# Matmul order in two places: column groups in turn for the first conditioning blocks, row halves in turn for the state-space outputs

## The chip, the core and the metric

The kernel runs on one core of one Trainium2 chip. The metric is the device time of one execution in microseconds (us). An engine runs its own list of instructions in order and waits on semaphores for the others: TensorE (PE, matmuls; its weight loads are listed apart as PEld), VectorE (DVE), ScalarE (ACT), GpSimd (POOL) and SyncE (SP, which starts DMAs).
## The reference

Two layers work on 512 latent tokens and 256 context tokens of 1024 channels. Nine modulation vectors per layer come from a conditioning vector, for latent and for context:

```python
mod_lat = (silu(c) @ w_ada[l] + b_ada[l])        # 9 vectors of 1024
mod_ctx = (silu(c_ctx) @ w_ada[l] + b_ada[l])
x = _post(x, _swiglu(_pre(x, g[0], mod_lat, 0), ffn1_gu[l], ffn1_down[l]), g[1], mod_lat, 0, 0.5)
h = _pre(x, g[2], mod_lat, 1) @ w_in[l]
y_ssm = _s5_mixer(h[..., :512], ...)             # 32 groups of 16 channels, 64 complex states each, both directions
y_f = _fnet(h[..., 512:], w_fmix[l])
x = _post(x, concat(y_ssm, y_f) @ w_out[l], g[3], mod_lat, 1, 1.0)
x = _post(x, _swiglu(_pre(x, g[4], mod_lat, 2), ffn2_gu[l], ffn2_down[l]), g[5], mod_lat, 2, 0.5)
```

`_pre` normalises, scales and shifts by two of the vectors; the context stream goes the same way with `mod_ctx` (not after layer 1's mixer). So the first feed-forward block can't begin before the first vectors of layer 0 are there.

## The kernel before

**The plan.** Channels lie on partitions, tokens on the free dimension. PE carries out six sections: feed-forward, mixer, feed-forward for each layer. Most of its time goes into line 434, where a product in high precision is made of three matmuls of high and low parts. Ahead of the first section stands a start: constants, loading x, transposes, the sums of squares (line 807), and then the first conditioning blocks.

**Conditioning blocks ("rides").** The 72 columns of 128 modulation values of a layer are made in blocks of three columns (RIDE = 3). The first eight blocks (FIRST_RIDES, 24 columns) are made at the start, by `ada_ride` (line 522), which `start_tensor` (line 1648) calls for R = 0 to 7. In one block, 24 matmuls have the two conditioning vectors as weights (`siluC[:, k, :]`, 128 partitions by 2 columns) and 128 columns of `w_ada` as moving data; column j of the block gets its result on PSUM partitions 32j and 32j+1, summed over the eight values of k. After each block but the first, PE transposes the rows of the block before (`ada_turn`, line 531); ACT copies a block's rows out of PSUM (`take_rows`, line 536, shown as L544) and takes the turned columns (L550). POOL issues the loads of `w_ada` (line 1646, 1536 KB each); blocks 6 and 7 reuse the buffers of blocks 0 and 1, so their loads wait until those are used. ACT then writes `hH` (line 841), DVE `hL` (line 903), and the first matmul of the feed-forward block waits for it (line 434 by way of `first_groups`, line 451). The other blocks are made later on DVE and don't change.

**The mixer's readout.** The 32 state-space groups go in four quarters q of eight groups. A quarter goes through these steps:

- `state_inputs(q)` (PE, line 1194): 32 matmuls with 128 partitions and 64 result partitions, the two column halves in turn.
- `turn(q)` (DVE, line 1491): takes them out of PSUM (L1513), and scans over the chunks (L1527, L1528). For q of 2 and over it first waits for POOL's part of quarter q-1 (`states_im`, line 1504).
- `turn_back(q)` (DVE, line 1534) makes the real part of the states, POOL (`mix_pool`, line 1024; L1078, L1079, L1082) the imaginary part.
- `outputs(q)` (PE, line 1198): for each half g2 of the partitions and each pair p of four, five matmuls into one PSUM region: one by `Tz` over all 128 partitions (line 1213), and four by `Ws` over the 64 partitions of half g2 (lines 1216 and 1217: real and imaginary part, both directions). Both halves have PSUM banks of their own. It waits for `states`, `states_im`, the loads of `Ws` and `Tz`, and the bank being free.
- `take_y(q)` (ACT, line 1324) copies the result out, sends it through DRAM and back, and the sums, the GELU and a gate follow.

PE's order is `state_inputs(q+1)`, then `outputs(q)`, for q = 0 to 3. In layer 1 the context part is left out: 64 moving columns in place of 96 in `outputs`. What the names in the rows stand for: `UC` chunks of the mixer's input, `SR`, `SI` and parts of `raw` the states, `VTs`, `Ws`, `Tz`, `Es` matrices made earlier in the section and loaded back.

Of the kernel before, what the change touches and what calls it, by code (L numbers as in the profile page):

```python
# [27 lines left out]
KC = D // 128  # L28
# [7 lines left out]
NST = 64  # L36
T8 = 8
NCH = TOK // T8
# [3 lines left out]
QP = NPAIR // HC  # L42
# [5 lines left out]
RIDE = 3  # L48
# [16 lines left out]
def build(nc, x, c, ctx_in, c_ctx, w_ada, b_ada, norm_g, ffn1_gu, ffn1_down, ffn2_gu, ffn2_down, w_in, w_out,  # L65
# [6 lines left out]
    def sb(name, shape, kb, dt=f32):  # L72
        return nc.alloc_sbuf_tensor_at(name, shape, dt, offset=BASE + int(kb * K))

    def sem(name):
        return stack.enter_context(nc.semaphore(name))
# [96 lines left out]
    Ws = [sb("Ws0", [128, 2, QT, 128], 122), sb("Ws1", [128, 2, QT, 128], 162)]  # L173
    VTs = [sb("VTs0", [128, 2, QT, 128], 130), sb("VTs1", [128, 2, QT, 128], 148)]
    Tz = [sb("Tz0", [128, QG, 128], 138), sb("Tz1", [128, QG, 128], 176)]
    Es = [sb("Es0", [128, 2, QT, NCH], 142), sb("Es1", [128, 2, QT, NCH], 156)]

    UC = [sb(f"UC{q}", [128, QG, NCH], kb) for q, kb in enumerate((204, 170, 173, 57))]
# [12 lines left out]
    ps = stack.enter_context(nc.psum_tensor("ps", [128, 8, 512], f32))  # L191
# [81 lines left out]
    rows = sem("rows")  # L273
# [155 lines left out]
    def three(pairs, dst, first, last):  # L429

        n = 0
        for wh, wl, xh, xl in pairs:
            for a, b in ((wh, xh), (wh, xl), (wl, xh)):
                ins = nc.tensor.matmul(dst, a, b, start=first and n == 0, stop=last and n == 3 * len(pairs) - 1)  # L434
                n += 1
        return ins
# [85 lines left out]
    def ada_ride(pe, R, bank, col):  # L522

        pe.wait_ge(ada_first[R % 6], 16 * (R // 6 + 1))
        for j in range(RIDE):
            for k in range(KC):
                ins = nc.tensor.matmul(ps[32 * j:32 * j + 2, bank, col:col + 128], siluC[:, k, :],  # L527
                                       ada_early[R][:, k, j * 128:(j + 1) * 128], start=k == 0, stop=k == KC - 1)
        ins.then_inc(ada_used, 1)
# [483 lines left out]
    def states_of(M, q):  # L1013

        if q % 2 == 0:
            return SR, SI
        return [raw[:, (M.base + i) % RAW_SLOTS, 0:QT * NCH].rearrange("p (t c) -> p t c", c=NCH) for i in (12, 13)]
# [69 lines left out]
    def mix_tensor(pe, M, pre):  # L1088
        l, tok0 = M.layer, M.tok0
        pe.wait_ge(rows, M.n0["rows"] + ROWS)  # L1090
        for i in range(2):
            for a in range(4):
                ins = nc.tensor.transpose(ps[:, 4 + i, a * 128:(a + 1) * 128], crow[:, i, a, :], ident[:])
# [50 lines left out]
        for n in range(HC):  # L1144
            for a in range(2):
                col = (n % 2) * 256 + a * 128
                ins = nc.tensor.matmul(ps[:, n // 2, col:col + 128], headDft[:, a, :], fmixW[:, n, :], start=True, stop=True)
# [50 lines left out]
        def outputs(q):  # L1198

            s, c0 = q % 2, M.c0  # L1200
            re, im = states_of(M, q)
            pe.wait_ge(set_c[s], M.n0["set_c"] + SET_C * (q // 2 + 1))
            pe.wait_ge(states, M.n0["states"] + q + 1)
            if q:
                pe.wait_ge(states_im, M.n0["states_im"] + q)
            if q >= 2:
                pe.wait_ge(y_taken, M.n0["y_taken"] + q - 1)
            for g2 in range(2):
                rows = slice(g2 * NST, (g2 + 1) * NST)
                bank = 4 + 2 * (q % 2) + g2  # L1210
                for p in range(QP):
                    dst = ps[:, bank, p * NCH + c0:(p + 1) * NCH]
                    nc.tensor.matmul(dst, Tz[s][:, 2 * p + g2, :], UC[q][:, 2 * p + g2, c0:NCH], start=True, stop=False)  # L1213
                    for d in range(2):
                        t = d * QP + p
                        nc.tensor.matmul(dst, Ws[s][rows, 0, t, :], re[rows, t, c0:NCH], start=False, stop=False)  # L1216
                        ins = nc.tensor.matmul(dst, Ws[s][rows, 1, t, :], im[rows, t, c0:NCH], start=False, stop=d == 1)  # L1217
            ins.then_inc(y_ps, 1)

        channels(0)  # L1220
# [10 lines left out]
        for q in range(HC):  # L1231
            if q + 1 < HC:
                state_inputs(q + 1)
            outputs(q)
# [4 lines left out]
        for k in range(HC):  # L1239
            pe.wait_ge(g_lo, M.n0["g_lo"] + k + 1)  # L1240
            for m in range(HC):
# [3 lines left out]
                cols = slice((m % 2) * 128, (m % 2) * 128 + 128)  # L1245
                for i, (t0, w) in enumerate(halves(tok0)):
                    t0 -= tok0
                    ins = three([(wh[:, k, cols], wl[:, k, cols], gH[:, k, t0:t0 + w], gL[:, k, t0:t0 + w])],
                                ps[:, 2 * m + i, 0:w], k == 0, k == HC - 1)
# [398 lines left out]
    def start_tensor(pe):  # L1648
# [26 lines left out]
        for R in range(FIRST_RIDES):  # L1675
            if R >= 4:
                pe.wait_ge(ada_rows, R - 3)
            ada_ride(pe, R, R % 4, 0)
            if R:
                ada_turn(pe, R - 1, 4 + (R - 1) % 2, 128 * ((R - 1) // 2))  # L1680
# [254 lines left out]
```

## Time and profile before

| what | value |
|---|---|
| median of 3 runs | 3167.54 us (3165.77 to 3173.11) |
| profiled execution, first to last instruction (the span; no time around it is shown) | 3167.4 us |
| PE, PEld busy share of the span | 92%, 85% |
| DVE, ACT, POOL busy share | 55%, 22%, 12% |
| mean granted TensorE clock | 0.921 |
| DMA, mean | 99 GB/s |

PE is busy nearly all the time, and records of PE overlap: a group's busy time is how long at least one of its records ran, and the distance between the starts of two records tells more than their length. The granted clock is 1.00 (2.4 GHz) or 0.50 (1.2 GHz) at any one time; a value between them is the mean of a stretch.

### The profile page before, as it was taken

Reading aid. Unit: us, or ns where it says so; the run is one execution under the profiler, and the core shown is the slowest. Engines: PE = TensorE matmul, PEld = TensorE weight load, DVE = VectorE, ACT = ScalarE, POOL = GpSimd, SP = SyncE. Lnnn points to the kernel's source line nnn. Section 1 sums busy time; section 2 is a strip of 40 time slices with the busy share of each in tenths; the row PEclk is TensorE's granted clock in tenths of the full one; section 3 lists DMA queues with packets and bytes.
Section 4 is the critical chain, followed back from the end, with each engine's and each line's share of the span. In section 5 each row is a group of like instructions: output and inputs, shape, how many; then the busy total and the mean of one; then the engine's idle time right before and its main releaser. Section 6 shows DMA issues by size and latency. Waiting matters only on the chain.

```text
span 3167.4 us, 41582 instructions
## 1 busy us (share of the span) xinstructions
PE 2918.2 (92%) x16334; PEld 2700.8 (85%) x16334; DVE 1736.6 (55%) x2513; ACT 696.4 (22%) x921; POOL 389.4 (12%) x609
## 2 busy tenths in 40 slices
PE   7999999977989879999999799999977889799997
PEld 5999999966868869999999699999966668578886
DVE  4776757567444377666665733333367444554444
ACT  3311111132101331111112311111132101332222
POOL 1000000027703110000001000000027622100001
PEclk9999999987785989999999899999987686899998
DMA  7334343313353214333331122121213353223331
GB/s 250 122 104 137 101 139 99 99 40 119 121 174 100 57 62 132 119 119 119 119 119 53 35 66 66 60 62 57 73 40 110 130 192 79 67 80 93 99 94 52
DMA packets 343593, 313.84 MB, mean 99 GB/s; under 512 B 52544, under 2 KB 318664, under 8 KB 338888
## 3 DMA queue, kind: packets, MB, share of 16 engines
q1 hardware_dynamic: 280136, 204.59, 21.5%
q10 hardware_dynamic: 59264, 89.07, 8.5%
q0 software_dynamic: 4096, 18.88, 1.6%
q8 instruction: 62, 1.02, 0.1%
q14 instruction: 35, 0.29, 0.0%
HBM read 280.58 MB, written 31.92 MB: 99 GB/s over the span
## 4 chain that ended last, share of the span: by engine, by line
PE 81%; DVE 8%; POOL 4%; DMA 2%; ACT 2%; issue 1%; SPq 0%; ACTq 0%; DVEq 0%
PE ps L434 68%; PE ps L1131 2%; PE ps L560 2%; PE ps L807 1%; PE ps L1216 1%; PE ps L1177 1%; PE ps L1217 1%; PE ps L527 1%; PE ps L1194 1%; PE ps L1213 1%; DVE tmpN L885 1%; DMA E_d<-EG 1%; DVE rmsX L894 1%; DVE hL L903 1%; DVE xT L773 1%
## 5 line engine op out<-in xcount | busy, mean ns | idle before, releaser
L434 PE MATMUL ps<-hH,wH 128*128 128x384 f32 (+1 forms) x2880 | 1005.0, 349 | 68.0 <-DVE hL L903 46.4
L434 PE MATMUL ps<-hL,wH 128*128 128x384 f32 (+1 forms) x2880 | 998.4, 347 | 0.0
L434 PE MATMUL ps<-hH,wL 128*128 128x384 f32 (+1 forms) x2880 | 997.5, 346 | 0.0
L426 DVE TENSOR_TENSOR wL<-raw,wH 128x1024 fp32r<-128x1024 f32 x300 | 366.0, 1232 | 522.8 <-ACT wH L419 521.4
L434 PEld LDWEIGHTS ps<-hH,wH 128*128 128x128 f32 x2880 | 550.0, 191 | 91.3 <-issue 49.3
L434 PEld LDWEIGHTS ps<-hL,wH 128*128 128x128 f32 x2880 | 549.7, 191 | 18.0
L434 PEld LDWEIGHTS ps<-hH,wL 128*128 128x128 f32 x2880 | 549.0, 191 | 18.3
L419 ACT ACTIVATE wH<-raw 128x1024 fp32r<-128x1024 f32 x300 | 310.7, 1050 | 581.7 <-PE ps L434 577.7
L434 PE MATMUL ps<-midH,wH 128*128 128x384 f32 (+1 forms) x1232 | 423.6, 344 | 9.8 <-DVE wL L426 9.8
L434 PE MATMUL ps<-midL,wH 128*128 128x384 f32 (+1 forms) x1232 | 423.4, 344 | 0.0
L434 PE MATMUL ps<-midH,wL 128*128 128x384 f32 (+1 forms) x1232 | 423.2, 344 | 0.0
L708 DVE TENSOR_TENSOR yT<-ps,yT 128x768 f32<-128x768 f32 (+1 forms) x352 | 307.8, 887 | 144.2 <-PE ps L434 143.1
L519 DVE SCALAR_TENSOR_TENSOR adaW<-adaW,siluC 128x384 f32<-128x384 f32 x520 | 293.8, 610 | 1.4
L748 POOL TENSOR_TENSOR sumY<-sq 128x768 f32<-128x768 f32 (+1 forms) x6 | 10.8, 1798 | 2262.8 <-ACT sq L819 2262.8
L691 DVE TENSOR_TENSOR midF<-ps,sgate 128x768 f32<-128x768 f32 (+1 forms) x88 | 78.4, 890 | 360.4 <-PE ps L434 360.4
L434 PEld LDWEIGHTS ps<-midH,wH 128*128 128x128 f32 x1232 | 232.8, 189 | 18.3 <-DVE wL L426 11.2
L434 PEld LDWEIGHTS ps<-midH,wL 128*128 128x128 f32 x1232 | 232.9, 189 | 6.9
L434 PEld LDWEIGHTS ps<-midL,wH 128*128 128x128 f32 x1232 | 232.6, 189 | 6.7
L661 ACT ACTIVATE midH<-midF 128x768 fp32r<-128x768 f32 (+1 forms) x88 | 69.8, 793 | 564.3 <-DVE midF L691 564.3
L654 ACT ACTIVATE sgate<-ps 128x768 f32<-128x768 f32 (+1 forms) x88 | 66.8, 759 | 228.9 <-PE ps L434 214.4
L1131 PE MATMUL ps<-W,BbR 64*16 64x112 f32 x256 | 69.6, 372 | 43.4 <-DVE W L1459 41.5
L807 PE MATMUL ps<-sq,ones 128*128 128x512 f32 (+1 forms) x144 | 64.6, 596 | 19.6 <-ACT sq L829 19.5
(254 smaller groups left out, 2641.0 us busy)
## 6 DMA issues: line engine op xcount, KB each, us to landing
raw<-in_ffn_gu_dram SPq DMA_DIRECT2D x176, 512.0 KB, 3.8
adaW<-in_w_ada_dram ACTq DMA_DIRECT2D x40, 1536.0 KB, 6.8
raw<-in_ffn_down_dram SPq DMA_DIRECT2D x88, 512.0 KB, 3.7
raw<-in_w_in_dram SPq DMA_DIRECT2D x16, 512.0 KB, 4.3
VT_d<-VTm ACTq DMA_DIRECT2D x8, 1024.0 KB, 3.9
W_d<-W ACTq DMA_DIRECT2D x8, 1024.0 KB, 4.9
raw<-in_w_out_dram SPq DMA_DIRECT2D x16, 512.0 KB, 4.4
VTs<-VT_d SPq DMA_DIRECT2D x8, 1024.0 KB, 5.3
```

The costliest lines, as they stand in the source:

```text
L419: nc.scalar.activation(wH[:, n % SPLIT_SLOTS, :], raw[:, n % RAW_SLOTS, :], ACT.Copy).then_inc(w_hi, 1)
L426: nc.vector.tensor_tensor(wL[:, n % SPLIT_SLOTS, :], raw[:, n % RAW_SLOTS, :], wH[:, n % SPLIT_SLOTS, :].bitcast(f32), ALU.subtract).then_ ...
L434: ins = nc.tensor.matmul(dst, a, b, start=first and n == 0, stop=last and n == 3 * len(pairs) - 1)
L519: ins = stt(at, w[:, k], siluC[:, k, v:v + 1], adaP[:] if i == 3 else at, ALU.mult, ALU.add)
L527: ins = nc.tensor.matmul(ps[32 * j:32 * j + 2, bank, col:col + 128], siluC[:, k, :], ada_early[R][:, k, j * 128:(j + 1) * 128], start=k == ...
L560: ins = nc.tensor.matmul(ps[:, bank, col + 2 * j + v:col + 2 * j + v + 1], adaW[:, R % 2, 1 - v, j * 128:(j + 1) * 128], ones[:, 0:1], sta ...
L654: nc.scalar.activation(sb_pair(sgate[:, f % 2, :], F.tok0), ps_pair(2 * (f % 2), F.tok0), ACT.Silu)\
L661: nc.scalar.activation(midH[:, f % 4, F.tok0:TOK], midF[:, f % 2, F.tok0:TOK], ACT.Copy).then_inc(mid_hi, 1)
L691: nc.vector.tensor_tensor(sb_pair(midF[:, f % 2, :], F.tok0), ps_pair(2 * (f % 2) + 1, F.tok0), sb_pair(sgate[:, f % 2, :], F.tok0), ALU.m ...
L708: nc.vector.tensor_tensor(sb_pair(yT[:, m, :], F.tok0), ps_pair(m % 4, F.tok0), sb_pair(yT[:, m, :], F.tok0), ALU.add).then_inc(down_read, 1)
L807: ins = nc.tensor.matmul(seg_ps(6, 7, v), ones[:, 0:1].broadcast_to([128, 128]), N.sq[:, m, t0:t1], start=m == 0, stop=m == KC - 1)
L1131: ins = nc.tensor.matmul(ps[0:GH, bank, c0:c1], bt[rows, tile, :], rhs, start=n == 0, stop=n == len(terms) - 1)
```

## The change

In `ada_ride` the loops over j (the three columns) and k (the eight parts of the sum) change places. In `outputs` the loop over the two halves g2 goes from the outside to the inside, around each single product. No instruction is added or removed, and no wait or semaphore changes.

```diff
     def ada_ride(pe, R, bank, col):
 
         pe.wait_ge(ada_first[R % 6], 16 * (R // 6 + 1))
-        for j in range(RIDE):
-            for k in range(KC):
+        for k in range(KC):
+            for j in range(RIDE):
                 ins = nc.tensor.matmul(ps[32 * j:32 * j + 2, bank, col:col + 128], siluC[:, k, :],
                                        ada_early[R][:, k, j * 128:(j + 1) * 128], start=k == 0, stop=k == KC - 1)
         ins.then_inc(ada_used, 1)
...
-            for g2 in range(2):
-                rows = slice(g2 * NST, (g2 + 1) * NST)
-                bank = 4 + 2 * (q % 2) + g2
-                for p in range(QP):
-                    dst = ps[:, bank, p * NCH + c0:(p + 1) * NCH]
-                    nc.tensor.matmul(dst, Tz[s][:, 2 * p + g2, :], UC[q][:, 2 * p + g2, c0:NCH], start=True, stop=False)
-                    for d in range(2):
-                        t = d * QP + p
-                        nc.tensor.matmul(dst, Ws[s][rows, 0, t, :], re[rows, t, c0:NCH], start=False, stop=False)
-                        ins = nc.tensor.matmul(dst, Ws[s][rows, 1, t, :], im[rows, t, c0:NCH], start=False, stop=d == 1)
+            bank = 4 + 2 * (q % 2)
+            for p in range(QP):
+                cols = slice(p * NCH + c0, (p + 1) * NCH)
+                for g2 in range(2):
+                    nc.tensor.matmul(ps[:, bank + g2, cols], Tz[s][:, 2 * p + g2, :], UC[q][:, 2 * p + g2, c0:NCH],
+                                     start=True, stop=False)
+                for d in range(2):
+                    t = d * QP + p
+                    for a, part in ((0, re), (1, im)):
+                        for g2 in range(2):
+                            rows = slice(g2 * NST, (g2 + 1) * NST)
+                            ins = nc.tensor.matmul(ps[:, bank + g2, cols], Ws[s][rows, a, t, :], part[rows, t, c0:NCH],
+                                                   start=False, stop=d == 1 and a == 1)
             ins.then_inc(y_ps, 1)
```

In the order of PE's instructions the first edit can't be seen, since the 24 matmuls of a block read alike. The second can. This is the list of PE before, layer 0, from `state_inputs(1)` into the first half of `outputs(0)`; a row is one matmul with its result and operands, and the partitions of the result by the moving columns:

```order
L1194 MATMUL ps<-UC_134,VTs_128 64x96 x32
L1213 MATMUL ps<-UC_133,Tz_129 128x96
L1216 MATMUL ps<-SR,Ws_125 128x96
L1217 MATMUL ps<-SI,Ws_125 128x96
L1216 MATMUL ps<-SR,Ws_125 128x96
L1217 MATMUL ps<-SI,Ws_125 128x96
L1213 MATMUL ps<-UC_133,Tz_129 128x96
```

And this is the same place in the list of PE now (lines 1212 and 1219 are the two matmul statements):

```order
L1194 MATMUL ps<-UC_134,VTs_128 64x96 x32
L1212 MATMUL ps<-UC_133,Tz_129 128x96 x2
L1219 MATMUL ps<-SR,Ws_125 128x96 x2
L1219 MATMUL ps<-SI,Ws_125 128x96 x2
L1219 MATMUL ps<-SR,Ws_125 128x96 x2
L1219 MATMUL ps<-SI,Ws_125 128x96 x2
L1212 MATMUL ps<-UC_133,Tz_129 128x96 x2
```

Two blocks of five matmuls, which stood a whole half of the quarter apart, have become one block of ten, where each product stands twice in a row, first for the partitions 0 to 63 and then for 64 to 127. `Tz` and `Ws` follow each other four times in a quarter where it was eight times.

## Rows read from the trace of the kernel before

**Rows 1.** Page, chain that ended last: share of the span by line.

```profile
PE ps L434 68%; PE ps L1131 2%; PE ps L560 2%; PE ps L807 1%; PE ps L1216 1%; PE ps L1177 1%; PE ps L1217 1%; PE ps L527 1%; PE ps L1194 1%; PE ps L1213 1%; DVE tmpN L885 1%; DMA E_d<-EG 1%; DVE rmsX L894 1%; DVE hL L903 1%; DVE xT L773 1%
```

**Rows 2.** Windows of both last quarters' outputs: engines' busy us (instructions), clock, DMA, GB/s.

```profile
1001.80:1022.80 21.00, 21.00 (x81) 18.26 (x81) 3.71 (x4) 3.04 (x4) 0.00 (x0) 0.50 0.08 20
2655.10:2675.20 20.10, 20.09 (x81) 18.21 (x81) 2.65 (x4) 2.19 (x4) 0.00 (x0) 0.50 0.10 22
```

**Rows 3.** Timeline of the first blocks: start, us, engine, line, count, idle before.

```profile
43.33 8.48 PE L527 MATMUL ps<-adaW,siluC 128*2 128x128 f32 x96
44.38 2.95 ACT L419 ACTIVATE wH<-raw 128x1024 fp32r<-128x1024 f32 x3
47.90 0.83 ACT L544 ACTIVATE modrow<-ps 2x128 f32<-2x128 f32 x3 [0.57 <-PE ps L527]
48.16 0.88 POOL L1646 DMA_DIRECT2D adaW<-in_w_ada_dram  x1 [21.84 <-PE ps L527]
52.00 4.54 PE L527 MATMUL ps<-ada_early,siluC 128*2 128x128 f32 x48
...
56.47 0.33 PE L534 MATMUL ps<-ident,modrow 128*128 128x128 f32 x1
56.73 4.54 PE L527 MATMUL ps<-ada_early,siluC 128*2 128x128 f32 x48
```

**Rows 4.** Timeline of PE: records within 43.33 to 44.60, then 44.64 to 45.00.

```profile
43.33 1.47 PE L527 MATMUL ps<-adaW,siluC 128*2 128x128 f32 x12
...
44.42 0.82 PE L527 MATMUL ps<-adaW,siluC 128*2 128x128 f32 x10
```

**Rows 5.** Line 1646, loads of w_ada at the start.

```profile
DMA to landing us min/median/max: 7.8/11.8/21.8
```

**Rows 6.** Timeline of PE, 960.2 to 960.9: state inputs, column halves in turn.

```profile
960.00 1.07 PE L1194 MATMUL ps<-UC,VTs 128*64 128x96 f32 x22
```

**Rows 7.** Timeline of PE, 751.0 to 751.4: line 1131 goes from row half to row half.

```profile
751.20 0.18 PE L1131 MATMUL ps<-CTr,BbR 64*16 64x16 f32 x1
751.21 0.36 PE L1131 MATMUL ps<-W,BbR 64*16 64x112 f32 x1
751.23 0.18 PE L1131 MATMUL ps<-CTr,BbR 64*16 64x16 f32 x1
```

**Rows 8.** Timeline of PE: one block of outputs(0), layer 0, and the next.

```profile
939.45 0.46 PE L1216 MATMUL ps<-SR,Ws 64*128 64x96 f32 x2
939.75 0.38 PE L1217 MATMUL ps<-SI,Ws 64*128 64x96 f32 x2
939.97 0.38 PE L1216 MATMUL ps<-SR,Ws 64*128 64x96 f32 x2
...
940.90 0.46 PE L1216 MATMUL ps<-SR,Ws 64*128 64x96 f32 x2
```

**Rows 9.** Timelines of POOL, DVE and PE, layer 0's readout.

```profile
955.29 2.32 POOL L1082 TENSOR_TENSOR raw<-raw,zp 128x380 f32<-128x380 f32 x3
961.29 0.56 DVE L1513 TENSOR_TENSOR za<-ps,Es 128x384 f32<-128x384 f32 x1 [7.74 <-PE ps L1194]
977.57 2.78 POOL L1082 TENSOR_TENSOR SI<-SI,zp 128x380 f32<-128x380 f32 x3
981.85 0.56 DVE L1513 TENSOR_TENSOR za<-ps,Es 128x384 f32<-128x384 f32 x1 [2.61 <-PE ps L1194]
1001.79 0.71 PE L1213 MATMUL ps<-UC,Tz 128*128 128x96 f32 x2 [3.39 <-POOL raw L1082]
```

**Rows 10.** Timelines of POOL and DVE, layer 1's readout.

```profile
2607.03 2.32 POOL L1082 TENSOR_TENSOR raw<-raw,zp 128x380 f32<-128x380 f32 x3
2612.41 0.56 DVE L1513 TENSOR_TENSOR za<-ps,Es 128x384 f32<-128x384 f32 x1 [7.13 <-PE ps L1194]
2629.51 2.32 POOL L1082 TENSOR_TENSOR SI<-SI,zp 128x380 f32<-128x380 f32 x3
2635.45 0.56 DVE L1513 TENSOR_TENSOR za<-ps,Es 128x384 f32<-128x384 f32 x1 [8.49 <-PE ps L1194]
```

## The prediction

> **What bounds the kernel now.** I read the page's chain of waits first: PE's line 434 holds 68% of it, but lines 527, 1213, 1216 and 1217, which the change touches, stand on it too, with about a percent each [rows 1]. Such lines can be worth more or less than their share, so I read their stretches one by one.
>
> At the start, PE does the eight blocks with no gap: blocks 0 and 1 as 96 records from 43.33, then a block, a transpose, a block. From the first record of block 2 to the transpose behind it is 56.47 - 52.00 = 4.47 us, and from block to block 4.73 us [rows 3]. The first feed-forward block waits for the columns, so PE is the bound here.
>
> In the readout of the mixer two bounds alternate. DVE's `turn(q)` sits idle 2.6 to 8.5 us for PE's state inputs, which stand behind the outputs of the quarter before; but POOL's last operation ends not long before, and PE in turn waits 3.39 us for POOL ahead of layer 0's last outputs [rows 9, 10]. Behind the last quarter nothing covers PE: 21.0 us in layer 0, 20.1 us in layer 1, both wholly at a granted clock of 0.50, the lower level [rows 2]. So the last outputs count in full, and the earlier ones only until POOL and DVE are the bound.
>
> **The blocks at the start.** A block has 48 records, sixteen for each of its three column groups, and two borders between groups; blocks 0 and 1 together have 96 and five. Let a record start d behind the one before it in its group and last L, and let b records at each border run beside records of the group before. Three rows give 11d + L = 1.47, (47 - 2b)d + L = 4.54 and (95 - 5b)d + L = 8.48 [rows 3, 4], which b = 4, d = 0.109 and L = 0.27 us solve. The border itself agrees: ten records within 0.82 us, where twelve inside a group take 1.47 [rows 4]. So different column groups run at the same time, as deep as PE looks ahead, and a block now takes 40 places of 0.109 us (blocks 0 and 1: 76).
>
> After the change a group gets two records, then the next group has its turn. For all three to be at work PE must look past one waiting record of each, three in all, and that is what it does at a border (the fourth of the last four is running). Then the three groups run side by side and a block takes 16 places, 1.74 us. Three at once is nowhere in this trace, only two; two at once would be 24 places. I take three, since nothing in the border's rows limits it to a pair. Saved: six blocks at 24 places, 15.7 us, and 76 - 32 = 44 places, 4.8 us, for the first pair: 20.5 us.
>
> The Trainium skill (TensorE: Matmul & The Clock Gate, Measured speedup vs the span model) gives 2.38, not 3, for matmuls on three column groups. By it a block would be 48 x 0.109 / 2.38 = 2.2 us, and the end 3.6 us later than in the sum below: 3123 us, an estimate from that page. No row here shows three groups.
>
> What is late next: the transpose of block 0 needs ACT's copy, and ACT is busy with splitting weights until 44.38 + 2.95 = 47.33. It then needs 0.83 us [rows 3], so the transpose is at about 48.25, where PE would be ready at 46.9. That costs 1.35 us, once. Later copies of 0.83 us fit into a cycle that was 56.73 - 52.00 = 4.73 us and loses 24 x 0.109: 2.1 us. Block 2 then starts at 48.25 + 0.26 = 48.5 (0.26 is from transpose to block, 56.47 to 56.73), block 6 at 56.9, block 7 at 59.0. The loads: block 6's was issued at 48.16, when block 0 was done, and comes 24 places earlier, to 45.6; landing took between 7.8 and 21.8 us [rows 3, 5]. At the short end it lands at 53.4, in time. Block 7's is issued at about 47.1, so it may take 11.9 us, about the median of the row; each us more is lost. I count it as in time. Gain at the start: 20.5 - 1.35 = 19.2 us; all that follows (ACT's and DVE's first h, the feed-forward block) is the same chain, only earlier.
>
> **The outputs.** Five matmuls, ten records, take 940.90 - 939.45 = 1.45 us at the full clock; the records of `Ws` follow each other at (939.97 - 939.75) / 2 = 0.11 us [rows 8]. The pass over 96 columns needs only 0.109 x 96/128 = 0.08, so the load of 128 weight columns sets this pace. Ten records are 1.12 us, so the two changes between 128 and 64 partitions cost 0.33 us together. In the new order a pair p, both halves together, has four records of `Tz` and sixteen of `Ws`, with two changes instead of four. That row halves run at the same time is shown at line 1131: a record of the second half starts 0.01 us behind one of the first half, and ahead of another of the first half that stands before it in the list [rows 7]. Those have weights of 16 columns; whether two loads of 128 columns, one for each half, run at once isn't in the trace. The nearest row is that of the column halves, with 64 weight columns each: 22 records within 1.07 us, under 0.05 us each, where one pass takes 0.08, so there loads and passes of two halves lie beside each other [rows 6]. I take it for the row halves too. A pair is then 4 + 16/2 = 12 places of 0.111, plus 0.33: 1.66 us for 2.90, a ratio of 0.57. The other end, loads one after the other, is 20 places: 2.55 us, a ratio of 0.88.
>
> Last quarters: 21.0 x 0.57 = 12.0 and 20.1 x 0.57 = 11.5, that is 9.0 and 8.6 us saved, if the clock stays at 0.50 as in the rows. If it rose for the whole stretch, four pairs would take 6.6 us and save another 5 us in each layer; PE will have waited some 8 us before these outputs, so I keep the low clock.
>
> Earlier quarters: `turn(2)` can't start before POOL's part of quarter 1, at 955.29 + 2.32 = 957.6; it starts at 961.3 now, so 3.6 us at most are gained. `turn(3)` starts at 981.85, POOL ends at 980.35: another 1.4 us. So layer 0's last outputs start 5.0 us earlier, and PE's shorter outputs are hidden behind POOL [rows 9]. Layer 1: 2612.4 - 2609.4 = 3.0 and 2635.4 - 2631.8 = 3.6, less 0.1 for DVE's start: 6.5 us [rows 10]. PE is ready for that: outputs(1) from 957.8 at the low clock end at 970, state inputs at 975, and `turn(3)` is due at 976.8.
>
> **Sum.** 19.2 + (5.0 + 9.0) + (6.5 + 8.6) = 48.3 us. The profiled execution spans 3167.4 us, within 0.2 us of the median, so 3119 us.
>
> **Rivals.**
> (a) Loads of the row halves go one after the other. Outputs shrink to 0.88 only: the last quarters by 2.5 us each. PE stays the bound of two quarters before them; a quarter is eight times 1.45 = 11.6 us at the full clock, up to 21.0 at the low one, so each gives 1.4 to 2.5 us, about 4 us in a layer. That is 13 us in place of 29.1: 3135 us. For it: no row shows two loads of 128 columns at once. Against: rows 6.
> (b) Column groups don't run side by side, and the start keeps its time: 3167.4 - 29.1 = 3138 us. Two at a time would be the half of it: 24 places save 13.5 us, 3125 us. Against (b) stand the ten records of rows 4.
> The Trainium skill (TensorE: Matmul & The Clock Gate, The mechanism) says that weight loads overlap with matmuls in flight only where the row group differs, which is (b). The trace disagrees at the borders [rows 4].
> (c) The clock rises in the last outputs: 3109 us. For it: PE does more per time there; against: it comes out of a wait.
> (d) Slower: every change of group or half drains the array, at 0.165 us (half of 0.33). It decides as soon as nothing overlaps any more, whatever the drain costs: a block then has 48 places and 24 drains, 9.2 us for 4.4, 39 us in eight blocks; a pair p has ten changes in place of four, 1.0 us at the full and 1.8 us at the low clock, some 5.5 us per quarter and 44 us in eight quarters: 3250 us. Against it: rows 4 and 7 show changes that cost nothing.
> (e) Block 7's load takes 17 us or more, behind the feed-forward weights: 5 us and more lost, 3124 us. It is inside the range.
>
> **Chances.** The forecast with (e) and two at a time 0.62; (a) 0.14; (b) 0.06; (c) 0.13; (d) 0.03; nothing changes, since PE already orders this itself, 0.02. What can be told from no change is 0.2%, 6 us. Faster: all but (d) and the last, 0.95; same 0.02; slower 0.03. The range goes from (c), with some us for other stretches where the clock falls differently, to (b): 3106 to 3140.
>
> **What would show it.** In the new profile a block of line 527 should take about 2.0 us from its first record to the end of the last, with 48 records, and the first matmul of line 434 should start 19 us earlier. The last outputs should take near 12 us in each layer; PE should wait about 8 us for POOL before them, where it now waits 3.4 us in layer 0, and DVE should wait no more for PE's state inputs in quarters 2 and 3. Wrong would be: blocks of over 2.6 us (two groups at most), last outputs of 17 to 19 us at a clock of 0.50 (rival (a)), or a wait of PE for a DMA ahead of block 6 or 7.

## The result and the profile after

| | before | after |
|---|---|---|
| median | 3169.82 us (3165.77 to 3173.11, 4 runs) | 3120.56 us (3118.02 to 3123.8, 4 runs) |
| ratio | | 0.9843, 95% interval 0.983 to 0.9856 |
| span of the profiled execution | 3167.4 us | 3120.4 us |
| mean granted clock | 0.921 | 0.924 |

The forecast was 3119 us; the median fell by 49.3 us, 1.6%, and the interval of the ratio is clear of 1. The line numbers of the outputs are now L1212 (`Tz`) and L1219 (`Ws`); DVE's first operation of `turn` is L1516, POOL's load L1649.

The first blocks, PE's timeline (start, us, engine, line, count, idle before), to be held against [rows 3]:

```profile
42.65 0.61 PE L527 MATMUL ps<-adaW,siluC 128*2 128x128 f32 x12
...
51.88 1.92 PE L527 MATMUL ps<-ada_early,siluC 128*2 128x128 f32 x48
...
53.99 2.00 PE L527 MATMUL ps<-ada_early,siluC 128*2 128x128 f32 x48
```

Twelve records lie within 0.61 us here, within 1.47 us in [rows 4]. A block of 48 records takes 1.92 us for 4.54, and from block to block it is 53.99 - 51.88 = 2.11 us for 4.73. By the prediction's model, 15 further places of 0.109 and one record of 0.27 make 1.91. How three groups lie side by side shows in a window of 45 ns at block 7's start:

```profile
58.60 0.28 PE L527 MATMUL ps<-adaW,siluC 128*2 128x128 f32 x3 [0.24 <-DMA adaW<-in_w_ada_dram]
```

Three records begin within those 45 ns; in one group a record begins 0.109 us behind the last. (The ends of matmul records are modelled in a profile, so the reading rests on the starts and on the length of the block.) But block 7 doesn't run through. Its last part, and the chain to the first feed-forward matmul:

```profile
58.60 1.91 PE L527 MATMUL ps<-adaW,siluC 128*2 128x128 f32 x44 [0.24 <-DMA adaW<-in_w_ada_dram]
62.09 0.39 PE L527 MATMUL ps<-adaW,siluC 128*2 128x128 f32 x4 [1.59 <-issue]
62.41 0.33 PE L534 MATMUL ps<-ident,modrow 128*128 128x128 f32 x1
63.71 0.47 PE L534 MATMUL ps<-ident,modrow 128*128 128x128 f32 x1 [0.97 <-ACT modrow L544]
66.73 0.66 PE L434 MATMUL ps<-hH,wH 128*128 128x384 f32 x1 [2.54 <-DVE hL L903]
```

After 44 records PE stands still for 1.59 us, and "issue" means that no wait in the profile explains it. Experiments 6 to 9 take this up.

The last outputs of layer 0, PE's timeline, and then the windows of both last quarters' outputs (engines' busy us and instructions, clock, DMA share, GB/s), against [rows 2]:

```profile
979.20 1.14 PE L1212 MATMUL ps<-UC,Tz 128*128 128x96 f32 x4 [8.90 <-POOL raw L1082]
980.27 2.03 PE L1219 MATMUL ps<-raw,Ws 64*128 64x96 f32 x16
982.23 1.17 PE L1212 MATMUL ps<-UC,Tz 128*128 128x96 f32 x4
```

```profile
979.20:991.46 12.26, 12.26 (x81) 10.89 (x81) 3.71 (x4) 3.04 (x4) 0.00 (x0) 0.50 0.01 1
2615.56:2627.39 11.83, 11.83 (x81) 10.89 (x81) 2.65 (x4) 2.19 (x4) 0.00 (x0) 0.50 0.02 4
```

The same 81 records take 12.26 us for 21.0 and 11.83 for 20.1, still at the lower clock. A pair takes 982.23 - 979.20 = 3.03 us.

DVE's waits of `turn(2)` and `turn(3)` in layer 0, and PE's `state_inputs(1)` in both layers with its last two waits in layer 1, against [rows 9, 10]:

```profile
939.44 0.56 DVE L1516 TENSOR_TENSOR za<-ps,Es 128x384 f32<-128x384 f32 x1 [4.18 <-POOL raw L1082]
959.26 0.56 DVE L1516 TENSOR_TENSOR za<-ps,Es 128x384 f32<-128x384 f32 x1 [5.01 <-POOL SI L1082]
```

```profile
917.75 2.86 PE L1194 MATMUL ps<-UC,VTs 128*64 128x96 f32 x64 [2.11 <-DVE hL L1490]
...
2554.63 2.86 PE L1194 MATMUL ps<-UC,VTs 128*64 128x96 f32 x64 [1.50 <-DVE hL L1490]
...
2596.01 1.07 PE L1212 MATMUL ps<-UC,Tz 128*128 128x64 f32 x4 [2.89 <-POOL SI L1082]
...
2615.56 1.09 PE L1212 MATMUL ps<-UC,Tz 128*128 128x64 f32 x4 [7.73 <-POOL raw L1082]
```

Where DVE waited for PE's state inputs, it now waits for POOL. From `state_inputs(1)` to the last outputs it is 61.45 us in layer 0 (917.75 to 979.20) and 60.93 in layer 1. Before, those state inputs began here (PE's timeline), and the last outputs are in [rows 2]: 67.1 and 67.3 us.

```profile
934.66 4.24 PE L1194 MATMUL ps<-UC,VTs 128*64 128x96 f32 x64 [2.11 <-DVE hL L1487]
...
2587.77 2.86 PE L1194 MATMUL ps<-UC,VTs 128*64 128x96 f32 x64 [1.50 <-DVE hL L1487]
```

Layer 0's `state_inputs(1)` took 4.24 us in the execution before and takes 2.86 us in this one: the clock differs there, and the account of the prediction below comes back to it.

The page's chain by line, against [rows 1]: line 527 and the outputs are no longer among the lines that it names, and POOL's product L1078 is.

```profile
PE ps L434 69%; PE ps L1131 2%; PE ps L560 2%; PE ps L807 1%; PE ps L1177 1%; DVE tmpN L885 1%; DMA E_d<-EG 1%; DVE rmsX L894 1%; DVE xT L773 1%; DVE hL L903 1%; DVE tmpN L911 1%; ACT wH L419 1%; POOL raw L1078 1%; DVE zb L1530 1%; DVE zd L
```

### The profile page after: what moved, and what is told of

Read it like the earlier page. It is cut to its first block, busy times and chain, and to the rows that moved or that the text cites. A ratio compares the mean times of both kernels' runs of the same rounds, so it can differ in the third digit from the quotient of the medians.

```text
span 3120.4 us, 41582 instructions
## 1 busy us (share of the span) xinstructions
PE 2833.4 (91%) x16334; PEld 2627.6 (84%) x16334; DVE 1733.7 (56%) x2513; ACT 696.0 (22%) x921; POOL 390.3 (13%) x609
## 4 chain that ended last, share of the span: by engine, by line
PE 78%; DVE 9%; POOL 6%; DMA 2%; ACT 2%; issue 2%; SPq 0%; ACTq 0%; DVEq 0%; POOLq 0%
PE ps L434 69%; PE ps L1131 2%; PE ps L560 2%; PE ps L807 1%; PE ps L1177 1%; DVE tmpN L885 1%; DMA E_d<-EG 1%; DVE rmsX L894 1%; DVE xT L773 1%; DVE hL L903 1%; DVE tmpN L911 1%; ACT wH L419 1%; POOL raw L1078 1%; DVE zb L1530 1%; DVE zd L1531 1%
```

## The experiments

Theory: different column groups of the array run side by side, three at a time, and so do the two row halves, loads of weights included; PE sees this only as far as it looks ahead, about four records; the last outputs count in full, the earlier ones until POOL and DVE are the bound. Rivals: the gain is that of fewer changes between 128 and 64 partitions; or one edit alone carries it all.

**1 and 2. Each edit alone.** The blocks with the outputs as before, then the outputs with the blocks as before (`for j` outside, `for k` inside).

> The first edit alone, the outputs as before. If both edits are worth what the trace of the changed kernel shows, the blocks give 16 to 18 us: 3151 us, first feed-forward matmul near 66.7, block 7 again with a gap of about 1.6 us; both readouts as before (last outputs 21 and 20 us). If the gain at the start were given back later (clock, weights arriving late), it would be under 10 us: 3158 or more.

> The second edit alone, the blocks as before. Expected 29 us: 3138 us, with last outputs near 12 us in each layer at the low clock, and the start as before (84 us). The two edits touch no common stretch, so the gains of this and of the first edit alone should add up to that of both within 2 us. If instead they shared something (the clock of later stretches), the sum would miss by 5 us or more.

Blocks alone: 3148.89 us (3146.33 to 3154.48, 5 runs), ratio 0.9937 (0.9915 to 0.9958). Outputs alone: 3143.88 us (3140.56 to 3145.18, 4 runs), ratio 0.9915 (0.989 to 0.994). The kernel before had 3169.27 beside them, so the gains are 20.4 us (16 to 18 expected) and 25.4 us (29 expected), together 45.8; the two edits in one gave 49.3. The sum misses by 3.5 us, between the 2 us and the 5 us of the two forecasts, and each interval reaches some 7 us either way, so the medians don't settle it. The traces do. With the blocks alone it is 66.73 - 43.00 = 23.7 us from block 0 to the first feed-forward matmul, and the last outputs take 21.0 and 20.15 us; with the outputs alone it is 40.9 us, 12.26 and 11.83. Each version has its own part as the changed kernel has it, and the other part as before.

**3. Halves in runs.** The order p, then `Tz` for both halves, but the four `Ws` matmuls of one half before those of the other.

```diff
-                for d in range(2):
-                    t = d * QP + p
-                    for a, part in ((0, re), (1, im)):
-                        for g2 in range(2):
+                for g2 in range(2):
+                    for d in range(2):
+                        t = d * QP + p
+                        for a, part in ((0, re), (1, im)):
```

> Blocks in the new order. Outputs: per pair p both Tz products, then all Ws products of half 0 (eight records), then all of half 1. The number of changes between 128 and 64 partitions is that of the changed kernel (two per pair). Theory: the halves run beside each other only as deep as PE looks ahead, four records at the border, so a pair has 4 + 16 - 4 = 16 places for 12: layer 0's last outputs take 12.2 x 16/12 less the fixed part, about 15.6 us. Rival: the gain came from the fewer changes; then 12.2 us as with halves in turn.

The time of one run was 3127.34 us (the kernel before, once beside this and the other single runs of 4, 6 and 7, took 3164.26). The windows of the last outputs:

```profile
979.27:995.37 16.10, 16.10 (x81) 14.73 (x81) 3.71 (x4) 3.04 (x4) 0.00 (x0) 0.50 0.01 1
2619.42:2634.88 15.46, 15.46 (x81) 14.52 (x81) 2.64 (x4) 2.19 (x4) 0.00 (x0) 0.50 0.04 8
```

This order has as few changes between 128 and 64 partitions as the changed kernel. It saves 4.9 of the 8.7 us in layer 0; the other 3.8 need the alternation. The rival alone would have left 12.2 us here. But it holds a part: the edit did two things, fewer changes (with one border per pair, where halves overlap) and row halves side by side. Eight changes fewer in a quarter are 1.5 us of the 4.9, an estimate by the 0.19 us of experiment 4; no run separates the rest.

**4. `Tz` first, and 5. only the last quarter.** All eight `Tz` matmuls of a quarter ahead of all `Ws`, so two partition changes per quarter are left of eight. And: the new order in quarter 3 alone, the old one in quarters 0 to 2.

```diff
                     nc.tensor.matmul(ps[:, bank + g2, cols], Tz[s][:, 2 * p + g2, :], UC[q][:, 2 * p + g2, c0:NCH],
-                                     start=True, stop=False)
+                                     start=p == 0, stop=False)
+            for p in range(QP):
+                cols = slice(p * NCH + c0, (p + 1) * NCH)
                 for d in range(2):
```

> Both edits, and the Tz products of a quarter all first, so two changes between 128 and 64 partitions in a quarter for eight. A pair at the low clock takes 3.05 us, 12 places of 0.214 and 0.48 for its two changes; six changes less are 1.45 us in each last quarter: 12.2 to 10.8 and 11.8 to 10.3 us. The time falls by 3 us, which one look can't tell. If the 0.48 us were not the change but the loads of Tz, the last outputs stay at 12 us.

> Blocks in the new order; outputs in the new order for the last quarter of each layer alone, quarters 0 to 2 in the order of before. Theory: the last quarter counts in full (8.8 and 8.3 us), the three before it only until POOL is the bound, 5 to 6 us a layer: 11 to 12 us slower than with all quarters changed, 3132 us. Rival: each quarter's outputs stand on the path; then three quarters a layer at 5 to 8 us each are lost, 3150 us or more.

The windows of the last outputs with `Tz` first:

```profile
981.06:991.12 10.06, 10.06 (x81) 9.79 (x81) 3.71 (x4) 3.04 (x4) 0.00 (x0) 0.55 0.01 2
2620.97:2631.64 10.67, 10.66 (x81) 10.44 (x81) 2.65 (x4) 2.19 (x4) 0.00 (x0) 0.50 0.01 2
```

In layer 1, at the same clock, 11.83 - 10.67 = 1.16 us for six changes, where 1.45 was expected: 0.19 us each. (In layer 0 the clock is 0.55, so part of its gain is the clock.) That the loads of `Tz` are the price, which would have left 11.8 us, is out. Yet its one time, 3124.55 us, is no better. Part of it went back at once. The gate's last matmuls wait for the same way of the result through ACT and DRAM, and PE now idles longer before them and runs them colder: the 24 records took 4.44 us at a granted clock of 1.00 in the changed kernel's trace, 5.95 us at 0.72 with `Tz` first. From their first record to the feed-forward block behind, first of the changed kernel, then with `Tz` first:

```profile
1007.58 0.44 PE L434 MATMUL ps<-gH,wH 128*128 128x384 f32 x1 [1.70 <-DVE gL L1585]
1021.88 0.69 PE L434 MATMUL ps<-hH,wH 128*128 128x384 f32 x1 [9.86 <-DVE hL L1601]
```

```profile
1007.36 0.69 PE L434 MATMUL ps<-gH,wH 128*128 128x384 f32 x1 [3.55 <-DVE gL L1587]
...
1023.07 0.69 PE L434 MATMUL ps<-hH,wH 128*128 128x384 f32 x1 [9.76 <-DVE hL L1603]
```

14.30 us became 15.71 us: of 2.2 us won in layer 0, 1.4 are gone some 30 us later. Both traces of the version in 10 to 12, which has `Tz` first too, show the same (3.49 and 3.10 us idle, then 15.7 us). But a second trace of the changed kernel, after 1.78 us idle, has 15.19 us, so not all of the 1.4 need be the edit's. The rest is the spread between executions (below).

Only the last quarter: 3136.03 us (3132.67 to 3140.83), ratio 0.9896 (0.987 to 0.9922); 3132 was expected, and 3150 or more by the rival. PE's state inputs and last outputs in layer 1, and DVE's earlier waits there:

```profile
2558.69 2.86 PE L1194 MATMUL ps<-UC,VTs 128*64 128x96 f32 x64 [1.50 <-DVE hL L1502]
...
2626.15 1.08 PE L1213 MATMUL ps<-UC,Tz 128*128 128x64 f32 x4 [2.34 <-POOL raw L1082]
```

```profile
2583.28 0.56 DVE L1528 TENSOR_TENSOR za<-ps,Es 128x384 f32<-128x384 f32 x1 [7.08 <-PE ps L1194]
2606.47 0.56 DVE L1528 TENSOR_TENSOR za<-ps,Es 128x384 f32<-128x384 f32 x1 [8.64 <-PE ps L1194]
```

DVE waits for PE as in [rows 10], and PE waits 2.34 us, not 7.73. So the last quarter gives 3148.89 - 3136.03 = 12.9 us by the medians (17.0 by the windows), and the rest, 15.5 us by the medians, comes from quarters whose outputs are hidden now. The traces give less for these: in layer 1 6.5 us (`state_inputs(1)` to last outputs 67.46 us here, 60.93 in the changed kernel), as forecast; in layer 0 64.16 for 61.45, so 2.7 us of the forecast 5.0. The medians, with intervals this wide, don't settle the split; that the rival is out they do show.

**6 and 7. How far PE looks ahead.** Each group gets two matmuls (four records), then four (eight records), before the next has its turn.

```diff
-        for k in range(KC):
-            for j in range(RIDE):
+        for k, j in [(k0 + i, j) for k0 in range(0, KC, 2) for j in range(RIDE) for i in range(2)]:
```

> Outputs in the new order. Blocks: two values of k (four records) for a column group, then the next group. If each group has a line of waiting records of its own, a run of four fills one group's place and its line, the next two groups start at once, and a block takes 16 places as with runs of two: 1.9 us. If PE holds three waiting records in all, the third group starts two places late and a block takes 18 places: 2.15 us. Two groups at most would be 24 places, 2.8 us.

> Outputs in the new order. Blocks: four values of k (eight records) for a column group, then the next. A group's last four records run beside the next group's first four, at five borders in a block: 48 - 20 = 28 places, 3.05 us and a cycle of 3.4 us; six blocks are 6 x 1.3 us longer than in turn. The gap of 1.6 us in block 7 of the changed kernel: if PE ran out of instructions there since it went through its list faster than they were loaded, it is smaller or gone at this slower pace; if the data of block 7 were late, it is gone too, but then the row of the gap would name the load.

PE's timeline with runs of four, then with runs of eight:

```profile
56.77 1.94 PE L527 MATMUL ps<-adaW,siluC 128*2 128x128 f32 x48
...
59.02 1.92 PE L527 MATMUL ps<-adaW,siluC 128*2 128x128 f32 x44
62.30 0.60 PE L527 MATMUL ps<-adaW,siluC 128*2 128x128 f32 x4 [1.35 <-issue]
```

```profile
62.91 3.24 PE L527 MATMUL ps<-adaW,siluC 128*2 128x128 f32 x48
...
66.34 3.24 PE L527 MATMUL ps<-adaW,siluC 128*2 128x128 f32 x48
```

Runs of four cost nothing (1.94 us; 3120.14 us in all), runs of eight bring back half of the loss (3.24 us, between 1.92 and 4.54; 3134.14 us). In places, 1.94 us is 16, and 3.24 us is 28 (27 x 0.109 + 0.27 = 3.21), as forecast from four records at each of five borders; the forecast 3.05 us only left out how long the last record runs. With runs of four the third group starts behind six waiting records of the other two; three in all would have made 18 places, 2.12 us. With runs of eight the next group has to wait until four records of a run are left. What fits both, and the four records at a border from which the prediction started [rows 4], is a limit for each group, three records waiting behind the one that runs. That is worked out from these runs, not seen in one.

The gap behind record 44 is at the same place with runs of four, where other matmuls stand there, and is missing in the slower version. Shortly ahead of PE's return there is a 16 KB transfer of the instruction queue. In the changed kernel it is this row of the DMA view from 59.4 to 60.7 us (packets, MB, share of 16 engines' time); 5.6% of 16 x 1.3 us is 1.16 us:

```profile
q8 instruction: 1, 0.02, 5.6%
```

It landed at 60.6 (59.4 + 1.16), and PE resumed at 62.09. So I took it that PE had run out of instructions, and moved its instruction stream.

**8 and 9. Moving the stream.** 8 and then 58 small matmuls, results unused, where PE waits for x at the start.

```diff
         ins.then_inc(s_parps, 1)
+        for i in range(8):
+            nc.tensor.matmul(ps[0:16, 0, 0:16], ident[:, 0:16], ident[:, 0:16], start=True, stop=True)
         pe.wait_ge(s_xin, 32)
```

> The changed kernel with eight small matmuls (16 columns by 16 columns, two records each, results unused) put on PE while it waits for x at 14.7 us, so that everything behind them stands 16 records later in PE's instruction stream. In question is the 1.59 us gap of PE behind the 44th of block 7's 48 records, where the profile names nothing that it waits for, and after which it resumes some 1.5 us behind the landing of a 16 KB transfer of the instruction queue. Theory A, PE has run out of fetched instructions: the gap belongs to a place in the stream, so it comes 16 records earlier in block 7, behind about 28 of them, with about 1.5 us. Theory B, it belongs to what block 7 does or reads: it stays behind the 44th record. By both the time from block 0's first record to the first feed-forward matmul stays about 24.1 us and the span near 3120.

> The same with 58 small matmuls, 116 records, in the same idle time of PE. If a record and its weight load take 64 bytes each, 16 KB hold 128 records; a shift by 116 records then puts a border of the fetch 12 records later than in the changed kernel, that is behind block 7's last record and under the waits for ACT (0.97 us) and DVE (2.54 us) that follow. Theory A (stream runs out): block 7 has 48 records without a gap, about 1.9 us, and from block 0's first record to the first feed-forward matmul it is 22.5 us in place of 24.1. Theory B: the gap stays behind the 44th record, 24.1 us. The span moves by no more than a few us either way.

PE's timeline with 8 more, then with 58 more:

```profile
55.33 1.92 PE L527 MATMUL ps<-ada_early,siluC 128*2 128x128 f32 x48 [0.81 <-issue]
...
59.55 1.26 PE L527 MATMUL ps<-adaW,siluC 128*2 128x128 f32 x28
62.29 1.03 PE L527 MATMUL ps<-adaW,siluC 128*2 128x128 f32 x20 [1.48 <-issue]
```

```profile
59.99 1.92 PE L527 MATMUL ps<-adaW,siluC 128*2 128x128 f32 x48 [0.35 <-DMA adaW<-in_w_ada_dram]
61.84 0.33 PE L534 MATMUL ps<-ident,modrow 128*128 128x128 f32 x1
63.15 0.33 PE L534 MATMUL ps<-ident,modrow 128*128 128x128 f32 x1 [0.97 <-ACT modrow L544]
66.02 0.66 PE L434 MATMUL ps<-hH,wH 128*128 128x384 f32 x1 [2.54 <-DVE hL L903]
```

Sixteen records earlier in the stream, the gap comes behind record 28: 44 - 16. And a second one, 0.81 us, shows in front of block 5, that is 28 + 48 + 48 records and two transposes earlier: 126 records. That is about one transfer of the instruction queue: from 639.5 to 1009.5 us of the changed kernel's trace PE has 1909 records, and the queue brings 15 transfers (DMA view), so 127 records each:

```profile
q8 instruction: 15, 0.25, 0.3%
```

In the changed kernel the place 126 records ahead of the gap lies in block 5, and block 5 takes 2.00 us there, and up to 2.42 us in other traces, where its neighbours take 1.92. All nine traces with groups in turn or in runs of four and nothing put in ahead have the gap behind record 44, with 1.1 to 1.6 us, and PE resumes 1.3 to 1.6 us behind the landing of a transfer. With 58 more, block 7 runs through. From block 0's first record, at 44.01, to the first feed-forward matmul it is then 22.0 us (22.5 expected), not 24.1. So the gap belongs to the stream, and theory A holds. The spans, 3124.2 and 3123.0, tell nothing of 2 us: the same 4530 or so records between the start and layer 0's mixer took 819.28 us in one execution of the changed kernel and 814.12 in another (the windows of the two, columns as above):

```profile
66.73:886.01 819.28, 769.40 (x4533) 739.29 (x4533) 516.04 (x728) 171.64 (x224) 137.38 (x257) 0.93 0.35 110
```

```profile
66.27:880.39 814.12, 762.36 (x4532) 733.45 (x4532) 516.36 (x728) 171.62 (x224) 137.44 (x257) 0.94 0.36 111
```

**10 to 12. Taking up the new bound.** POOL now ends last in every quarter, with two products and a sum. So DVE takes over the second product and the sum of the imaginary part, and POOL keeps the first product; `Tz` first is in it too.

```diff
 # POOL: of its three steps only the first product is left
-            plink(pool, tt(zp[:], zb[:], e[:, 1], ALU.mult))
-                ins = tt(im[:, ts, cols], im[:, ts, cols], zp[:, ts, j0:j1], ALU.add)
 # DVE, behind turn_back of the real part
+            dlink(dve, tt(zp[:], zb[:], Es[q % 2][:, 1], ALU.mult))
+            dve.wait_ge(im_first, M.n0["im_first"] + q)
+                ins = tt(im[:, ts, cols], im[:, ts, cols], zp[:, ts, j0:j1], ALU.add)
```

> Both edits, and two things more. The Tz products of a quarter all come first, so that 128 and 64 partitions change twice a quarter and not eight times. And of the imaginary part of quarters 1 to 3, POOL makes only the first product; the second product and the sum go to DVE, which sat idle 4 to 5 us there. If POOL is the bound of the readout's cycle, a cycle shrinks by 2 to 3 us (POOL's 9.2 us to about 6.5), three in each layer, and the last outputs by 1.5 us: 16 to 20 us less than the changed kernel, 3102 us. If POOL was not the bound, only the 3 us of the outputs: 3118 us.

> The version with DVE making the second product and the sum of the imaginary states, timed again beside the changed kernel on the same chip. Theory: POOL's and DVE's cycle of a quarter is the bound of the readout after the change (19.6 us in layer 1's trace, 17.3 us in this version's), six us in each layer, plus some 2 us for the last outputs: 3110, with a range of 3104 to 3114, and 8 to 14 us below the changed kernel. Rival: the gap between the two was mostly the run-to-run spread of the clock in the stretches before: less than 4 us below it.

> The changed kernel itself, as the yardstick for the version above: 3120.6, 3118 to 3124, as timed first; ratio to the kernel before 0.983 to 0.986.

First 3110.27 us (3104.03 to 3114.17), ratio to before 0.9814 (0.9789 to 0.9839), where 3102 was expected. Then, timed beside each other on one chip: this version 3109.1 us (3104.64 to 3113.89, 5 runs), ratio 0.9809 (0.979 to 0.9828); the changed kernel 3122.06 us (3117.69 to 3125.13, 5 runs), ratio 0.9851 (0.9834 to 0.9868). The ranges of the runs and the intervals don't meet, and 13 us lie between the medians: the fastest of the kernels here. DVE's timeline in layer 1 of this version, and PE's:

```profile
2582.50 0.95 DVE L1580 TENSOR_TENSOR zp<-zb,Es 128x768 f32<-128x768 f32 x1
2583.48 1.09 DVE L1586 TENSOR_TENSOR SI<-SI,zp 128x380 f32<-128x380 f32 x3
2584.70 0.56 DVE L1515 TENSOR_TENSOR za<-ps,Es 128x384 f32<-128x384 f32 x1
```

```profile
2584.83 2.67 PE L1209 MATMUL ps<-UC,Tz 128*128 128x64 f32 x16 [1.77 <-DVE SI L1586]
2602.04 3.65 PE L1209 MATMUL ps<-UC,Tz 128*128 128x64 f32 x16 [7.52 <-DVE raw L1586]
```

DVE now goes from one quarter to the next without waiting. Its quarter is 2602.04 - 2584.83 = 17.2 us, against 2615.56 - 2596.01 = 19.6 in the changed kernel, where DVE and POOL took turns. The bound has become DVE alone. From `state_inputs(1)` to the last outputs each layer is 6.7 us shorter (54.71 and 54.18 us), and the last outputs 2.3 and 1.2 us; of these 16.9 us the medians show 13, and where the rest went stays open.

## Why the prediction was right

| term (us) | predicted | measured |
|---|---|---|
| start, block 0 to first feed-forward matmul | 19.2 | 40.94 - 24.08 = 16.9 |
| layer 0, earlier quarters | 5.0 | 67.1 - 61.4 = 5.7 |
| layer 0, last outputs | 9.0 | 21.0 - 12.26 = 8.7 |
| layer 1, earlier quarters | 6.5 | 67.3 - 60.9 = 6.4 |
| layer 1, last outputs | 8.6 | 20.1 - 11.83 = 8.3 |
| sum | 48.3 | 46.0; the spans differ by 47.0 |

(40.94 is from 43.33 of [rows 3] to 84.27, where the first feed-forward matmul began before.) The missing 1.0 us is the sum of differences in stretches that the change doesn't touch: 0.7 us won ahead of block 0 (42.65 for 43.33) and 1.8 between the two readouts, 0.6 lost ahead of layer 0's and 0.8 behind layer 1's. One such stretch differed by 5 us between two executions of the changed kernel (above), so that sum, spans and medians (49.3) lie this close is partly luck.

**Three groups at once: shown.** The model of places (48 records, b = 4, d = 0.109) gave 16 places for a block, and 1.92 us is 16 places. The step from a pair at a border, which the trace had, to three at once, which it had not, held; two at a time would have made some 2.8 us. The Trainium skill (TensorE: Matmul & The Clock Gate, Measured speedup vs the span model) has 2.38 for three column groups; here the groups take 16 places for the 48 of one after the other, 3 times less. (That 4.54 / 1.92 is 2.36 doesn't confirm the 2.38, since the 4.54 us already hold eight places of overlap.) The rule of the Trainium skill in the same page's section The mechanism, that weight loads overlap with matmuls in flight only where the row group differs, doesn't hold for these blocks: their groups differ in columns alone, and 48 loads lie within the 1.92 us. That section of the Trainium skill also lets loads run ahead into a background weight buffer; no run here shows whether that is what happens.

**Row halves at once: shown.** Sixteen records of `Ws` take 2.03 us at the lower clock, four pairs 12.26 against the forecast 12.0. With the halves in runs they take 16.10. So two loads of 128 columns do lie beside each other, which no row of before had shown, and rival (a), 17 to 19 us, is out. The ratio 0.57 was right for a mixed reason, as in the forecast's own working: eight places fewer, and two partition changes fewer per pair.

**What is late next: right in kind.** PE waits 8.90 us and 7.73 us for POOL before the last outputs (about 8 was forecast), and DVE waits for POOL in `turn(2)` and `turn(3)`. The size in layer 0 was too large, and the table's 5.7 us hides it. In some executions the clock falls in layer 0's `state_inputs(1)`, in others not, whatever the order: the 64 records take over 4.2 us or 2.86. Here are two, the blocks alone and the changed kernel with 58 matmuls more:

```profile
916.83 2.86 PE L1194 MATMUL ps<-UC,VTs 128*64 128x96 f32 x64 [2.11 <-DVE hL L1487]
...
914.78 4.51 PE L1194 MATMUL ps<-UC,VTs 128*64 128x96 f32 x64 [2.11 <-DVE hL L1490]
```

From there to the last outputs the old order takes 67.1 us where the clock fell (the kernel before) and 64.1 or 64.2 where it didn't (blocks alone; last quarter alone). The new order takes 63.1 where it fell (outputs alone; 58 matmuls more; 63.0 with 8 more) and 61.4 where it didn't (the changed kernel, in two traces). Like against like that is 4.0 or 2.7 us; the rest of the 5.7 is the clock, and luck. The step that was mis-sized is POOL's second end: it was taken from the old trace, but POOL's first product of quarter 2 (L1078) became slower; first before, then now:

```profile
971.49 3.52 POOL L1078 TENSOR_TENSOR SI<-zd,Es 128x380 f32<-128x380 f32 x3 [13.88 <-DVE zd L1528]
949.64 5.21 POOL L1078 TENSOR_TENSOR SI<-zd,Es 128x380 f32<-128x380 f32 x3 [10.33 <-DVE zd L1531]
```

So `turn(3)` gained 0.7 us over `turn(2)`, not 1.4; `turn(2)` itself gained 3.3 us, where the clock fell, for the forecast 3.6. Why the product is slower was not tested.

**The start: 2.3 us too much.** The step that failed is "all that follows is the same chain, only earlier", together with block 7's load "in time". The load came 0.24 us late. And PE, over twice as fast through its instructions (2.11 us a block for 4.73), ran out of them in block 7. From that block's first record to its transpose it is 62.41 - 58.60 = 3.81 us, and 61.84 - 59.99 = 1.85 with 58 matmuls more: 1.96 us for the idle time of 1.59 and a new start. Together that is 2.2 of the 2.3 us. The version without the gap gains 40.94 - 22.01 = 18.9 us, near the forecast. The wait for ACT ahead of block 0's transpose was 1.08 us, for the forecast 1.35.

**The clock stayed low** in both last outputs (0.50), so rival (c) didn't come. Rivals (b) and (d) are out by the blocks' 1.92 us, and of rival (e), 5 us, no more than the 0.24 us came.

## What to carry to other kernels

Matmuls that use different column groups, or different row halves, of the array run side by side if they stand near each other in PE's list: for the column groups here runs of up to four records did as well as runs of two, while runs of eight, of column groups or of row halves, overlapped at their borders alone. A profile shows it before any change, at the borders between groups: count how many records fit into a stretch there. Then ask for each stretch what ends it: behind a last quarter a faster PE counts in full, in the middle it only moves the wait, here to POOL, and the next step is the split between POOL and DVE.

## What the runs showed of the hardware that was not expected

- PE can starve for instructions: 1.59 us in one place, 0.81 us in another, at 126 records' distance, and the place moves with the stream by exactly the 16 records put in ahead; PE gets 16 KB of instructions for every 127 records or so. Before the change, with a block of 4.54 us, the profile had no such gap.
- Three records in three column groups begin within 45 ns, and a block of three groups takes 16 places, as many as one group has records: the other two cost nothing.
- A shorter stretch of PE can make the next one colder: 1.85 us more idle time before the gate's last matmuls (3.55 for 1.70), a granted clock of 0.72 for 1.00 in them, and 1.4 us more in them and behind them.
